# Moving three weight splits and the constant copies of layer 0 (and one split of layer 1) to other places in VectorE's and ScalarE's order

## The reference

```
h = modulate(rmsnorm(x, n1), sh1, sc1)            # sh1, sc1 from silu(c) @ w_ada
a_q, a_k, a_v, b_q, b_k, b_v, z, xbc, dt_raw = split(h @ w_in)      # 1024 x 2320
o_a = attention(a_*)   o_b = attention(b_*)       # two groups of heads
o_c = mamba_mix(z, xbc, dt_raw, ...)              # conv of 3 taps, silu, chunked SSD scan
x = x + g1 * (concat(o_a, o_b, o_c) @ w_out)
x = x + g2 * hier_moe(modulate(rmsnorm(x, n2), sh2, sc2))            # 16 experts, top 1 group, top 2 in it
```

## Time and profile before

| | |
|---|---|
| time, median of 3 runs | 813.16 us (813.13 to 813.4) |
| the profiled execution's own time | 816.95 us |
| its span in the trace | 815.2 us |
| mean granted TensorE clock | 0.978 |
| PE busy | 768.5 us (94%) |
| DVE busy | 575.8 us (71%) |
| ACT busy | 483.4 us (59%) |
| POOL busy | 49.7 us (6%) |

### The profile page before, as it was taken

One profiled execution on the slowest core, in us unless ns is written; L12 is line 12 of the kernel. 1 busy time (PEld: TensorE's weight loads), 2 busy tenths in 40 slices (PEclk: granted clock), 3 DMA queues, 4 the chain that ended last, 5 costly groups with the idle time before them and its releaser, 6 DMA issues.

```text
span 815.2 us, 10925 instructions
## 1 busy us (share of the span) xinstructions
PE 768.5 (94%) x4044; PEld 583.1 (72%) x4044; DVE 575.8 (71%) x936; ACT 483.4 (59%) x796; POOL 49.7 (6%) x36
## 2 busy tenths in 40 slices
PE   4997999989999999999999999998999999999995
PEld 2565877456876788888776687754597788888874
DVE  3129678686526799999763767858663778999965
ACT  3023884476435877778533378546643687777752
POOL 0000551000000000000000046100000000000000
PEclk9998998999999999999999999899999999999998
DMA  9951122888407899999853111385742079999912
GB/s 368 416 196 53 52 90 92 331 341 303 162 6 306 327 380 377 362 380 362 326 208 120 52 53 45 130 345 178 263 160 95 1 261 379 361 383 371 364 47 81
DMA packets 33489, 186.00 MB, mean 228 GB/s; under 512 B 5136, under 2 KB 6288, under 8 KB 16400
## 3 DMA queue, kind: packets, MB, share of 16 engines
q1 hardware_dynamic: 33424, 185.17, 60.3%
HBM read 182.53 MB, written 2.62 MB: 227 GB/s over the span
## 4 chain that ended last, share of the span: by engine, by line
PE 84%; DVE 8%; ACT 3%; issue 3%; DMA 1%; DVEq 0%; ACTq 0%; SPq 0%
PE psum L806 22%; PE psum L921 11%; PE psum L835 11%; PE psum L1123 8%; PE psum L892 7%; PE psum L658 4%; PE psum L858 3%; PE psum L784 2%; PE psum L1005 1%; PE psum L739 1%; DVE att L2046 1%; PE psum L884 1%; PE psum L699 1%; PE psum L684 1%; PE psum L991 1%
## 5 line engine op out<-in xcount | busy, mean ns | idle before, releaser
L1841 DVE TENSOR_TENSOR split<-ring,split 128x2048 fp32r<-128x2048 f32 x96 | 219.8, 2290 | 33.2 <-ACT split L1410 31.8
L1410 ACT CAST split<-ring 128x2048 fp32r<-128x2048 f32 x96 | 183.6, 1912 | 25.3 <-PE psum L835 14.4
L806 PE MATMUL psum<-split,y_hi 128*128 128x512 f32 x512 | 160.8, 395 | 0.4 <-ACT selT L1383 0.4
L806 PEld LDWEIGHTS psum<-split,y_hi 128*128 128x128 f32 x512 | 93.7, 188 | 18.6 <-issue 0.4
L806 PE MATMUL psum<-split,y_lo 128*128 128x512 f32 x256 | 100.1, 391 | 0.0
L921 PE MATMUL psum<-ring_r,hT_hi 128*128 128x512 f32 x216 | 76.1, 407 | 0.0
L835 PE MATMUL psum<-split,hidT 128*128 128x512 f32 x256 | 69.7, 394 | 1.8 <-DVE hidT_lo L1846 1.8
L892 PE MATMUL psum<-hT,ring 128*128 128x384 f32 x192 | 70.6, 507 | 0.0
L835 PEld LDWEIGHTS psum<-split,hidT 128*128 128x128 f32 x256 | 47.3, 188 | 14.2 <-DVE hidT_lo L1846 4.8
L2263 POOL TENSOR_TENSOR ud<-const,da_hi 128x1024 fp32r<-128x1024 f32 x12 | 30.7, 2578 | 434.4 <-DVE da_lo L1939 433.9
L806 PEld LDWEIGHTS psum<-split,y_lo 128*128 128x128 f32 x256 | 48.0, 188 | 10.2
(11 more groups left out here) (284 smaller groups left out, 1356.0 us busy)
## 6 DMA issues: line engine op xcount, KB each, us to landing
ring<-in_w_gu SPq DMA_DIRECT2D x64, 1024.0 KB, 5.1
ring<-in_w_ada SPq DMA_DIRECT2D x40, 1024.0 KB, 6.6
ring<-in_w_down SPq DMA_DIRECT2D x32, 1024.0 KB, 5.2
ring<-in_w_rows SPq DMA_DIRECT2D x12, 1024.0 KB, 5.0
ring<-in_first SPq DMA_DIRECT2D x8, 1024.0 KB, 14.4
ring<-in_w_out SPq DMA_DIRECT2D x8, 1024.0 KB, 5.0
ring<-in_w_xbc SPq DMA_DIRECT2D x8, 784.0 KB, 8.4
par<-in_par SPq DMA_DIRECT2D x1, 1632.0 KB, 9.9
```

The lines of the kernel that those rows point to most:

```text
L806: last = pe.matmul(dst, x[:, g, t, :], w[:, j, :], start=(t == 0 and i == 0), stop=(t == KD - 1 and i == 2))
L1410: act.copy(splits[unit_split(n)][:, 0, :], slot(key)).then_inc(raised("whi", l, p), 1)
L1841: tt(lo, slot(unit_key(l, p, n)), hi.bitcast(F32), ALU.subtract).then_inc(raised("wlo", l, p), 1)
```

## The change

Four edits of order; no instruction is added or removed, and the data are the same.

1. VectorE, layer 0: the five constant copies become `tables()`, called in the norm behind chunk 5.
2. VectorE and ScalarE, layer 0: the splits of pieces 0 and 1 go into the norm, both behind chunk 6 (ScalarE: behind its copy for chunk 6). They were behind chunk 7.
3. VectorE, both layers: the remainder of piece 2 goes from ahead of the x/B/C step to behind its first group. ScalarE's cast of piece 2 stays.
4. The counts of `in_hi` and `in_lo` follow the new order, by layer.

```
-        IN_HI = {name: n + 1 for n, name in enumerate(("w0", "h0", "w1", "h1", "w2", "w3", "w4", "w5"))}
+        IN_FRONT = (("w0", "w1", "h0", "h1"), ("w0", "h0", "w1", "h1"))
+        IN_HI = [{name: n + 1 for n, name in enumerate(front + ("w2", "w3", "w4", "w5"))} for front in IN_FRONT]
...
# ScalarE, layer 0's loop over the eight copies
                                 act.copy(ada_rows[:, 0:2 * P], bank(key)[:, 0:2 * P]).then_inc(*was_read(key))
+                                if j == KD - 2:
+                                    for p in range(2):
+                                        split_win(0, p)
...
                     elif kind == "w_split":
-                        split_win(l, arg[0])
+                        if l or arg[0] > 1:
+                            split_win(l, arg[0])
...
# VectorE, the norm's loop over the chunks
                         ins.then_inc(sig["h"], 1)
+                        if not (l or n) and c == KD - 3:
+                            tables()
+                        if not (l or n) and c == KD - 2:
+                            for p in range(2):
+                                split_win(0, p)
+
+            def tables():
+
+                dve.wait_ge(const_in, 16)
+                dve.tensor_copy(ident_b, c_("ident"))
+                dve.tensor_copy(sides[:, 0, :], c_("after"))
+                dve.tensor_copy(sides[:, 1, :], c_("before"))
+                dve.tensor_copy(mask_b, const[:, C_MASK:C_MASK + 2 * DEC].rearrange("p (b k) -> p b k", b=2))\
+                    .then_inc(setup_dve, 1)
+                dve.wait_ge(par_in, 16)
+                ts(nsink, tab[:, :, T_SINK:T_SINK + NH], -1.0, None, ALU.mult).then_inc(dve_step, 1)
+                dve.wait_ge(dve_step, dve_steps())
...
                     elif kind == "w_split":
-                        split_win(l, arg[0])
+                        if l and arg[0] < 2 or arg[0] > 2:
+                            split_win(l, arg[0])
...
                     elif kind == "xbc":
-                        if l == 0:
-                            (the nine lines that are now tables())
...
                             stt(xbc[:, c, P:TOK - 1], src[:, P + 1:TOK], cw[2], xbc[:, c, P:TOK - 1],
                                               ALU.mult, ALU.add).then_inc(*was_read(key))
+                            if c == 0:
+                                split_win(l, 2)
```

More of the change, by code:

```diff
@@ L605, in spent @@
             return done[key][0], 1
-        IN_HI = {name: n + 1 for n, name in enumerate(("w0", "h0", "w1", "h1", "w2", "w3", "w4", "w5"))}
-        IN_LO = {name: n + 1 for n, name in enumerate(("w0", "h0", "w1", "h1", "w2", "h2", "w3", "w4", "w5"))}
+        IN_FRONT = (("w0", "w1", "h0", "h1"), ("w0", "h0", "w1", "h1"))
+        IN_HI = [{name: n + 1 for n, name in enumerate(front + ("w2", "w3", "w4", "w5"))} for front in IN_FRONT]
+        IN_LO = [{name: n + 1 for n, name in enumerate(front + ("w2", "h2", "w3", "w4", "w5"))} for front in IN_FRONT]
         def in_hi(l, name):
-            return sig["in_hi"], per["in_hi"] * l + IN_HI[name]
+            return sig["in_hi"], per["in_hi"] * l + IN_HI[l][name]
         def in_lo(l, name):
-            return sig["in_lo"], per["in_lo"] * l + IN_LO[name]
+            return sig["in_lo"], per["in_lo"] * l + IN_LO[l][name]
         def win_hi(l, p):
```

## The result

| | median | runs | ratio to the kernel before, 95% interval |
|---|---|---|---|
| kernel before | 813.14 us | 4 (811.79 to 813.4) | |
| changed kernel | 805.26 us | 4 (803.66 to 808.29) | 0.9895 (0.986 to 0.993) |

The ratio makes the change worth 8.5 us of 813.16, an expected 804.6: a little more than the 7.2 forecast, and 0.2 us outside the range of 804.8 to 808.9. The interval of the ratio, 801.8 to 807.5 us on the same scale, holds both the forecast of 806.0 and the range's lower end. The four runs of the changed kernel spread over 4.6 us, with mean granted clocks of 0.980, 0.989, 0.994 and 0.993 in the order 808.29, 805.65, 803.66, 804.88.

What follows compares the result with a forecast made beforehand. TensorE, busy 94% of the span, was taken as the bound, losing time to a layer 0 wait for VectorE and the slow clock behind it. 813.16 less 4.29 and 2.89 (7.18) gave 806.0 us, range 804.8 to 808.9.

Steps and rivals of the forecast that it cites:

- Idle time, 4.29 us: Layer 0, first row product: TensorE's wait for VectorE's read of the dt sums goes, winning 4.29 us.
- Slow clock, 2.89 us: Layer 0, thirteen row matmuls behind the wait at 1.2 GHz: full pace at once without idle time, winning 2.89 us.
- Layer 1 as a twin: Same code without the queue: 28.07 us from 12 records to first segment product, against layer 0's 35.25; difference 7.18.
- Rival 1: The slow clock stretch stays, there or a little later; only 4.29 us is won, 808.9 us; chance 8%.
- The covers: Moved work fits gaps at cost 0: 0.6 us spare before chunk 7, 2 on ScalarE, 0.4 at da.
- Signs: Right: no line 921 wait, line 991 near 90.8; wrong: waits at 978 or 991, later stages not all shifted 7.2 us.
- Third edit, expected 0: Piece 2's remainder behind the first x/B/C group, both layers: cost 0, bounds 0 to 1.0 us.
- the range's lower end: Whole kernel: 804.8 us, 1.2 below the forecast for run-to-run offset and a slightly larger slow-clock share.
- offset of the profiled execution: Profiled execution took 816.95 us, 3.8 over the runs' median; the same difference was taken off the forecast.
- Rival 2: The close deadlines are missed in both layers, 0.5 to 1 us each: 807.0 to 808.0 us; chance 10%.
- Rival 3: Another bank or piece holds the first row product at about the old time: 813 us, within 0.2%; chance 4%.
- Rival 4: Slower: TensorE waits for da in both layers, each wait starting a 2.89 us slow stretch; 815.2 us example; chance 3%.

Runs made afterwards that it cites:

- splits_only: Kernel before with only the splits of pieces 0 and 1 moved behind chunk 6; 809.84 us median of 10, ratio 0.9951.
- rest_only: Changed kernel with the splits of pieces 0 and 1 back behind chunk 7, only constants and piece 2's remainder moved; 811.51 us median of 12, ratio 0.9982.
- gap6_full: Changed kernel with the constant copies behind chunk 6, ahead of the two splits; 809.08 us in one run.
- gap_filled: Kernel before with six extra f32 products that nothing reads, filling TensorE's wait for the dt read; 815.55 us median of 12, ratio 1.0017.

## Why the prediction was right in its mechanism and too narrow in its range

- **Idle time, 4.29 us: right.** It is 4.29 in three traces of before and gone in four of the changed kernel. `splits_only` and `rest_only` each remove a part of it.
- **Slow clock, 2.89 us: right in kind, large in size.** Layer 1 as a twin gave the right end state (28.07 to 28.10 us in every trace), but the start state was taken from one trace. It measured 2.9, 1.7 and 1.8 us. What I had weighed against it from the Trainium skill ("TensorE: Matmul & The Clock Gate", What's actually happening), that the number of slow matmuls varies from run to run, the page says of the start of a kernel. In the middle of this one it held for the size: 13, 7 and 8 slow row products. It did not hold for whether the stretch comes: three times of three with the wait, never in four without. Rival 1, only 4.29 won, is refuted by the runs too (7.2 us with a standard error of 0.6). That a small part of it comes back near 112 us is not excluded.
- **The covers: right.** 0.58 us left before chunk 7, 2.22 us on ScalarE, slack behind that (`gap6_full`), 0.4 us at da (81.45 against 80.81 + 0.21 in the changed kernel, and 0.5 of wait with 0.94 more).
- **Signs.** No wait at lines 979 or 992 in either layer, none at 922 for the dt sums, a granted clock of 1.00 from 64 to 70 us, and layer 1's distance unchanged: as forecast. Line 992 at 90.8 and chunk 7 at 59.7 were not met (88.16 and 57.01), nor was the same shift of 7.2 us in the later stages (layer 1's 12 records start 9.75 us earlier). I had called the last a sign of being wrong; it came from the slow stretch at 18 to 23 us, which is no part of the edit. Such marks must be counted from a mark close by, as the distance is.
- **Third edit, expected 0: it is worth 0.5 us in layer 0.** I had not asked when piece 2's cast is ready for a VectorE that arrives 4.4 us earlier.
- **The step that failed is the range's lower end**, "from 1.2 below the forecast (run-to-run offset, a slightly larger slow-clock share)": the scatter was sized too small. I took the three runs of before, 0.3 us apart, for the scatter of this kernel. They were three like draws: 66 runs scatter over 9.5 us. The lower end allowed 1.2 us for this; the first comparison's own interval is about 3 us to either side. What I called an offset of the profiled execution (3.8 us over the median) was in part slow stretches, among them the one at 18 to 23 us. The page's clock row hides it (a 9 there is 90% or more); the row of that stretch, 0.76, shows it, and I did not ask whether it comes every time. A ratio from four runs on each side then lies a microsecond or two off the edit's worth by chance: 8.5, 5.4 and 8.1 us in three comparisons, 7.2 by all runs. That this is the forecast to a tenth is in part luck: the sum took the dearest of three slow stretches, and by the mean distance it would have been 6.4. The runs (7.2, standard error 0.6) can't tell the two apart.

Rivals 2, 3 and 4 did not come up. Neither did a loss in layer 1.

## What to carry to other kernels

Where two layers run the same code and only one has a wait, take the other as a ruler between two marks: in layer 1 that distance was 28.07 to 28.10 us in all 14 traces, while their times went from 805.5 to 817.0. With the wait in it the distance moved as well (34.05 to 35.25), so take it from more than one trace. Before giving a range, read the granted clock along the whole trace and ask of every slow stretch whether the next execution need have it; three equal times are no proof of a small scatter. When an engine's queue is shortened, check each instruction left in it for its own inputs: they were ready before only because the queue was long.

## What was not expected of the hardware

TensorE's 1.2 GHz stretches behind short waits are not a fixed property of a program. The same stage (second to third segment product of layer 0) took 19.42, 19.36, 17.45 and 17.45 us in four traces of one kernel: 2.0 us for the stretch, with the same 1.45 us wait for VectorE ahead of it. (The stretch slows TensorE by more: it also used up the 1.22 us in which TensorE otherwise waits for ScalarE.) Behind the 4.29 us wait the stretch came every time, at prices from 1.7 to 2.9 us; behind the 1.45 us wait it came in three of seven traces in layer 0 and in four of seven in layer 1. That this wait brings it is not shown. And removing a slow stretch in one place (`gap_filled`) did not lower the kernel's time.
